# Order of the block products at the quad border, and chunks of two and four FF pairs in the down projection

## Chip, cores, metric

One core of one Trainium2 chip. The metric is device time in microseconds (us) of one execution of the whole program, the median of several runs.

## The reference

One layer of a hybrid decoder on 512 prompt positions and 64 sample positions (8 sequences of 8), 576 columns in all, D_MODEL 2048, D_FF 5632, everything in float32:

```
h = rmsnorm(x); p = h @ w_in                      # 2048 x 5120
y_a = u * (tril(W_s) @ v + b_s); y_b = B * causal_dwconv3(C * x_B)
x = x + concat(group_rmsnorm(y_a), group_rmsnorm(y_b)) @ w_out
h = rmsnorm(x)
gate = causal_dwconv3(h @ w_gate)                 # 2048 x 5632
x = x + (silu(gate) * (h @ w_up)) @ w_down        # 5632 x 2048
y = rmsnorm(x)
```

Besides y the last two rows of each convolution's input and the normalised v of the samples are outputs. The change lies in the last two matrix products, the ConvFFN.

## The kernel before

**Split products.** TensorE multiplies in a rounded 32-bit format, so every float32 operand is split: hi is a rounded copy (ScalarE), lo the rest (VectorE), and each product is three matmuls, hi*hi, hi*lo, lo*hi, always 128x128 weights against 288 columns (HALF of the 576). The weights live in rings of four pieces (`w_hi`, `w_lo`; in the down projection `dw_hi`, `dw_lo`).

**Quads.** The first 4 of the 44 FF tiles are multiplied plainly (`std_quad`). The other 40 go through `quad(i, u)`: one tile of gate and up together by a block scheme with 7 products in place of 8. The 2x2 blocks of weights are a = gate rows of even k (`raw[:, 0]`), b = gate rows of odd k (`raw[:, 1]`), c and d = the same for up (`raw_c`, `raw_d`). VectorE makes the sums: `sum1` = c + d into `raw_e`, `sum2` = raw_e - a, `sum3` = a - c (in place of a), `sum4` = b - raw_e (in place of b). Product t uses `quad_form(t)` against `b_form(t)` and goes to one of four PSUM banks (b, b+1, b+2, b+3); banks of two quads alternate. ScalarE copies bank b after the first product that stands alone in it (`snap`, semaphore s1_done) and bank b+1 (into `up_sum`, s5_done) before later products add to them. `form_hi` (L1030) and `form_lo` (L1555) are the splits. Each is issued in a hand-written order on its engine:

- ScalarE `quad` (L1096): hi of forms 3 to 6 between silu, copies and the hi of the activations (`act_hi`), then hi of the next quad's forms 0, 1, 2.
- VectorE `quad` (L1660): `up2`, `c21`, lo 3, `sum3`, `times_gate`, act sums, lo 4, act_lo, lo 5, zpad, lo 6, act_lo, zpad, `sum1` of the next quad, `gate_conv`, lo 0, lo 1, `sum2`, lo 2, `sum4`.
- SyncE `quad_loads` (L446): raw_c when all four sums of the quad before are done, raw[:, 1] after its split 4, raw_d after split 5, raw[:, 0] after split 6. The very first quad loads raw[:, 0] early and, once std_quad 3 is half done, raw_c, raw_d, raw[:, 1].
- GpSimd (L618 to L674): the split activations of an FF pair (two tiles) are stored to DRAM (`act_scratch`) in four rounds per pair, in the seven forms that the down projection needs.

**Down projection.** It is the same 7-product scheme with the FF pairs as inner dimension. `CHUNKS` lists (first pair, number of pairs) of six chunks; each chunk has 8 visits, one for each two output tiles. Visit v makes 7 products of n pairs (n x 3 matmuls each), so 63 matmuls with three pairs and 84 with four. Each chunk needs seven activation forms, loaded from DRAM by GpSimd into 12 slots (`load_form`, L676, n x 288 KB each), and each visit a weight block loaded by SyncE (L475, n x 256 KB) into one of two buffers (`down_buf`; visit 0 has its own, `down_v0`, in the place of raw_e and after it). GpSimd makes the first and third weight sum (`sums13`, L690), VectorE the second and fourth (`down_s2`, `down_s4`) and seven splits `down_lo` (L1712); five VectorE instructions read the banks out (L1741 to L1770). From chunk 1 on GpSimd also adds copied banks to X (`snap_add`).

At the border between the last quad and visit 0 GpSimd issues the seven loads of forms as their slots come free:

```
for k, n in ((0, 1), (1, 1), (4, 2), (6, 2), (2, 3), (3, 3), (5, 4)):
    load_form(k, piece_done, N_LAST + n)
store_act(PAIRS - 1, 0)
sums13(0)
```

and SyncE the weights of visit 0 after split 4 of the last quad (`lo_ready >= N_LAST + 5`), those of visit 1 after split 6. In visit 0 TensorE also transposes the state rows (`states_t`, L2144), ScalarE copies them (`rows_stage`, L1148), and GpSimd writes them out ahead of its sums of visit 2 (L719). Forms 7 and 8 of the next chunk are loaded at visit 1, forms 9, 10, 11 at visit 2, 12 and 13 at visit 7, and the last pair's activations are stored at visits 2, 4, 6.

Of the kernel before, what the change touches and what calls it, by code (L numbers as in the profile page):

```python
# [22 lines left out]
F32R = mybir.dt.float32r  # L23
ALU = mybir.AluOpType
# [6 lines left out]
def build_layer(nc, x_prompt, x_sample, state_conv_mix, state_conv_ffn, norm_mix_g, w_in, sgu_norm_g,  # L31
# [21 lines left out]
    CHUNKS = ((0, 3), (3, 3), (6, 4), (10, 4), (14, 4), (18, 4))  # L53
# [16 lines left out]
    with ctx:  # L70
# [104 lines left out]
        slots = [sb(f"form{n}", [P, JM, 2, HALF], F32R, at=h_at + n * SLOT) for n in (0, 1, 2, 3, 9, 10, 8, 7, 6, 4, 5, 11)]  # L175
# [190 lines left out]
        def quad_form(t):  # L366

            return (raw[:, 0], raw_e[:, :, :], raw[:, 1], raw_e[:, :, :], raw[:, 1], raw_d[:, :, :], raw[:, 0])[t]
# [26 lines left out]
        def _(sp):  # L395
# [79 lines left out]
            for v in range(VISITS * len(CHUNKS)):  # L475
                f0, n, g = visit(v)
                if v == 0:
                    sp.wait_ge(stage_b_out, 16 * (PAIRS - 2))
                    sp.wait_ge(lo_ready, N_LAST + 5)
                else:  # L480
                    sp.wait_ge(lo_ready, D0 + NQ * (v - 1))
# [15 lines left out]
        def _(pool):  # L497
# [192 lines left out]
            def sums13(v):  # L690

                pool.wait_ge(down_landed[v % 2], 16 * (v // 2 + 1))
                if v == 1:
                    pool.wait_ge(piece_done, D0)
                g.tensor_tensor(down_sum(v), down_form(v, 6), down_form(v, 5), ALU.add).then_inc(s13_ready, 1)
# [16 lines left out]
            for k, n in ((0, 1), (1, 1), (4, 2), (6, 2), (2, 3), (3, 3), (5, 4)):  # L712
                load_form(k, piece_done, N_LAST + n)
            store_act(PAIRS - 1, 0)
            sums13(0)
            rows_ffn(FT - 1)
            for v in range(VISITS * len(CHUNKS)):
                ch, gv = v // VISITS, v % VISITS
                if v == 1:  # L719
                    pool.wait_ge(rows_staged, 1)  # L720
                    g.dma_start(new_ffn_prompt[0, 0].rearrange("r (t c) -> (r t) c", c=P), ffn_stage[0:2 * FT, 0, :]).then_inc(rows_out, 16)
                    rows = new_ffn_sample[0].rearrange("b k (t c) -> (b k t) c", c=P)
                    g.dma_start(rows[0:5 * P, :].rearrange("(n p) c -> p n c", p=P), ffn_stage[:, 1:6, :]).then_inc(rows_out, 16)
                    g.dma_start(rows[5 * P:2 * NB * FT, :], ffn_stage[0:2 * NB * FT - 5 * P, 6, :]).then_inc(rows_out, 16)
                    g.dma_start(new_mix_prompt[0, 0].rearrange("r (t c) -> (r t) c", c=P), mix_stage[0:16, 0, :]).then_inc(rows_out, 16)
                    g.dma_start(new_mix_sample[0].rearrange("b k (t c) -> (b k t) c", c=P), mix_stage[:, 1, :]).then_inc(rows_out, 16)
                if v == 2:
                    pool.wait_ge(rows_out, 5 * 16)
# [1518 lines left out]
```

## Time and profile before

| | |
|---|---|
| time, median of 3 runs | 2348.78 us (2340.26 to 2353.99) |
| the profiled execution | 2352.12 us |
| its span, first to last instruction | 2350.4 us, TensorE clock 0.99 granted |
| busy: TensorE, weight loads | 97%, 96% |
| busy: VectorE, ScalarE, GpSimd | 72%, 41%, 24% |
| quads | 888.9 to 1795.2 us |
| chunks 0, 1 of the down projection | 1803.4 to 1887.7, to 1955.5 us |
| DMA, mean | 136 GB/s |

Times are from the start of the span. Matmuls overlap in the profile: each is shown with some 0.29 us, while the next starts 0.13 us later, so a stretch is read by its length and the number of matmuls in it, not by busy time. PE is TensorE, DVE VectorE, ACT ScalarE, POOL GpSimd, SPq SyncE's queue of DMA issues. An engine's idle time is given before the instruction that it ended with, and what released it.

### The profile page before, as it was taken

To read this page: it belongs to the slowest core of one execution; us is meant where nothing else is said; L and a number is where in the kernel's file an instruction comes from. 1 tells how busy PE (TensorE), PEld (TensorE's weight loads), DVE (VectorE), ACT (ScalarE), POOL (GpSimd) and SP (SyncE) were. 2 spreads that over 40 slices of the span, in tenths; PEclk is the share of its full clock that TensorE was granted. 3 is DMA by queue.
4 is the path that set the end of the run, shared out by engine and by line. 5 is a ranking of instruction groups with operands and counts; after the bars stand their busy time and mean duration, and the time that the engine had idled before them with its cause. 6 is when DMAs were issued, how large, how long until landed. Compare 5 with 4: busy or idle time off the path is not lost. (4 is left out here: it accounts for less than half of the span.)

```text
span 2350.4 us, 43938 instructions
## 1 busy us (share of the span) xinstructions
PE 2276.6 (97%) x16978; PEld 2259.5 (96%) x16978; DVE 1688.3 (72%) x2281; ACT 971.4 (41%) x1469; POOL 555.5 (24%) x641
## 2 busy tenths in 40 slices
PE   7999999999999899999999999999998899999995
PEld 7999999999999899999999999999997899999995
DVE  6357744446322768787888888888886799888896
ACT  6224321223111444454444444444443454444454
POOL 2310000000222001111011111111113267656685
PEclk9999999999999999999999999999999999999998
DMA  7322233223433243534444344443435566765522
GB/s 245 98 81 60 73 86 90 75 86 112 155 105 101 73 137 115 163 116 149 129 140 155 113 158 129 135 147 127 152 123 210 175 218 223 235 204 191 175 86 99
DMA packets 368936, 320.09 MB, mean 136 GB/s; under 512 B 8648, under 2 KB 348739, under 8 KB 363072
## 3 DMA queue, kind: packets, MB, share of 16 engines
q1 hardware_dynamic: 346320, 203.98, 29.6%
q0 software_dynamic: 22512, 114.69, 13.0%
q8 instruction: 69, 1.13, 0.2%
q14 instruction: 35, 0.29, 0.0%
HBM read 258.32 MB, written 60.31 MB: 136 GB/s over the span
## 5 line engine op out<-in xcount | busy, mean ns | idle before, releaser
L1827 PE MATMUL ps<-h_hi,w_hi 128*128 128x288 f32 x1792 | 532.7, 297 | 2.2 <-issue 2.0
L1829 PE MATMUL ps<-h_hi,w_lo 128*128 128x288 f32 x1792 | 529.1, 295 | 0.0
L1828 PE MATMUL ps<-h_lo,w_hi 128*128 128x288 f32 x1792 | 528.9, 295 | 0.0
L2167 PE MATMUL ps<-form,dw_hi 128*128 128x288 f32 x1232 | 369.6, 300 | 23.6 <-DVE dw_lo L1715 21.0
L2168 PE MATMUL ps<-form,dw_hi 128*128 128x288 f32 x1232 | 365.0, 296 | 0.0
L2169 PE MATMUL ps<-form,dw_lo 128*128 128x288 f32 x1232 | 364.3, 296 | 0.0
L1827 PEld LDWEIGHTS ps<-h_hi,w_hi 128*128 128x128 f32 x1792 | 337.3, 188 | 3.5 <-issue 2.7
L1828 PEld LDWEIGHTS ps<-h_lo,w_hi 128*128 128x128 f32 x1792 | 337.2, 188 | 0.0
L1829 PEld LDWEIGHTS ps<-h_hi,w_lo 128*128 128x128 f32 x1792 | 337.1, 188 | 0.0
L1223 DVE TENSOR_TENSOR w_lo<-raw,w_hi 128x1024 fp32r<-128x1024 f32 x128 | 162.8, 1301 | 205.9 <-ACT w_hi L785 205.8
L1715 DVE TENSOR_TENSOR dw_lo<-down,dw_hi 128x512 fp32r<-128x512 f32 (+1 forms) x282 | 258.3, 928 | 51.9 <-ACT dw_hi L799 48.0
L2108 PE MATMUL ps<-hq,w_hi 128*128 128x288 f32 x960 | 286.0, 298 | 7.9 <-DVE w_lo L1560 7.8
L2109 PE MATMUL ps<-hq,w_hi 128*128 128x288 f32 x960 | 283.8, 296 | 0.0
L2110 PE MATMUL ps<-hq,w_lo 128*128 128x288 f32 x960 | 282.8, 295 | 0.0
L2167 PEld LDWEIGHTS ps<-form,dw_hi 128*128 128x128 f32 x1232 | 233.0, 189 | 27.6 <-issue 16.5
L2168 PEld LDWEIGHTS ps<-form,dw_hi 128*128 128x128 f32 x1232 | 234.9, 191 | 0.0
L2169 PEld LDWEIGHTS ps<-form,dw_lo 128*128 128x128 f32 x1232 | 234.6, 190 | 0.0
L785 ACT ACTIVATE w_hi<-raw 128x1024 fp32r<-128x1024 f32 x128 | 132.0, 1055 | 246.1 <-PE ps L1829 227.8
L1560 DVE TENSOR_TENSOR w_lo<-raw,w_hi 128x1024 fp32r<-128x1024 f32 x160 | 195.0, 1219 | 23.2 <-ACT w_hi L1043 23.2
L799 ACT ACTIVATE dw_hi<-down 128x512 fp32r<-128x512 f32 (+1 forms) x282 | 165.6, 593 | 110.2 <-PE ps L2169 88.2
L1043 ACT ACTIVATE w_hi<-raw 128x1024 fp32r<-128x1024 f32 x160 | 168.9, 1055 | 98.7 <-DMA raw<-in_w_gate_dram 70.7
L623 POOL DMA_DIRECT2D act_scratch<-stage x68 | 45.6, 670 | 642.5 <-DVE stage L1528 633.2
(289 smaller groups left out, 5195.3 us busy)
## 6 DMA issues: line engine op xcount, KB each, us to landing
raw<-in_w_gate_dram SPq DMA_DIRECT2D x88, 512.0 KB, 4.5
raw<-in_w_in_dram SPq DMA_DIRECT2D x80, 512.0 KB, 4.1
down<-in_w_down_dram SPq DMA_DIRECT2D x32, 1024.0 KB, 5.5
form<-act_scratch POOLq DMA_DIRECT2D x28, 1152.0 KB, 7.2
act_scratch<-stage POOLq DMA_DIRECT2D x46, 576.0 KB, 4.6
raw_c<-in_w_up_dram SPq DMA_DIRECT2D x40, 512.0 KB, 3.8
raw_d<-in_w_up_dram SPq DMA_DIRECT2D x40, 512.0 KB, 5.3
raw<-in_w_out_dram SPq DMA_DIRECT2D x32, 512.0 KB, 4.0
```

The lines of the kernel that those rows point to most:

```text
L1043: a.activation(w_hi[:, c], quad_form(t), ACT.Copy).then_inc(hi_ready, 1)
L1560: v.tensor_tensor(w_lo[:, c], quad_form(t), w_hi[:, c].bitcast(F32), ALU.subtract).then_inc(lo_ready, 1)
L1715: v.tensor_tensor(dw_lo[:, m % 4, 0:n], down_form(m // NQ, m % NQ), dw_hi[:, m % 4, 0:n].bitcast(F32), ALU.subtract).then_inc(lo_ready, 1)
L1827: te.matmul(out, whi, xhi, start=start, stop=False)
L1828: te.matmul(out, whi, xlo, start=False, stop=False)
L1829: return te.matmul(out, wlo, xhi, start=False, stop=stop)
L2108: te.matmul(out, w_hi[:, c, j, :], b_form(t, 0, j), start=start and j == 0, stop=False, skip_group_check=True)
L2109: te.matmul(out, w_hi[:, c, j, :], b_form(t, 1, j), start=False, stop=False, skip_group_check=True)
L2110: last = te.matmul(out, w_lo[:, c, j, :], b_form(t, 0, j), start=False, stop=stop and j == PJ - 1, skip_group_check=True)
L2167: te.matmul(out, dw_hi[:, m % 4, j, :], act_f[:, j, 0, :], start=start and j == 0, stop=False, skip_group_check=True)
L2168: te.matmul(out, dw_hi[:, m % 4, j, :], act_f[:, j, 1, :], start=False, stop=False, skip_group_check=True)
L2169: last = te.matmul(out, dw_lo[:, m % 4, j, :], act_f[:, j, 0, :], start=False, stop=stop and j == n - 1, skip_group_check=True)
```

## The change

Five things. (1) In a quad the first product is b's (`raw[:, 1]`, bank b+2), then a's and (c+d)'s; `sum1`, `sum2`, `sum4` follow in VectorE's order, `sum3` moves from behind split 3 to behind split 4 and, in even quads, act_lo and act_t4. SyncE's code of the quads is the same. (2) At the border SyncE asks for visit 0's weights after split 3 and `sum4`; GpSimd loads forms 0 and 1 and holds the other five until those weights have landed; the two sums of visit 0 are made by VectorE in the last quad, and `down_lo(3)` comes ahead of the last gate products. The first four slots are numbered so that forms 0 and 1 lie where b's product has read. (3) Chunks 0 and 1 have 2 and 4 pairs instead of 3 and 3: a visit has 42 and 84 matmuls, forms are 576 and 1152 KB, weights 512 and 1024 KB. (4) The state rows are transposed in visit 2 and written out in visit 4. (5) Forms 9, 10, 11 are loaded at visits 3, 4, 5, one each, and the last activations stored at visits 1, 3, 5.

```diff
@@ -50,7 +50,7 @@
     VISITS = KT // 2
-    CHUNKS = ((0, 3), (3, 3), (6, 4), (10, 4), (14, 4), (18, 4))
+    CHUNKS = ((0, 2), (2, 4), (6, 4), (10, 4), (14, 4), (18, 4))
@@ -172,7 +172,7 @@
         SLOT = JM * 2 * HALF * 4
-        slots = [sb(f"form{n}", [P, JM, 2, HALF], F32R, at=h_at + n * SLOT) for n in (0, 1, 2, 3, 9, 10, 8, 7, 6, 4, 5, 11)]
+        slots = [sb(f"form{n}", [P, JM, 2, HALF], F32R, at=h_at + n * SLOT) for n in (2, 3, 0, 1, 9, 10, 8, 7, 6, 4, 5, 11)]
@@ -365,7 +365,7 @@
-            return (raw[:, 0], raw_e[:, :, :], raw[:, 1], raw_e[:, :, :], raw[:, 1], raw_d[:, :, :], raw[:, 0])[t]
+            return (raw[:, 1], raw[:, 0], raw_e[:, :, :], raw_e[:, :, :], raw[:, 1], raw_d[:, :, :], raw[:, 0])[t]
@@ -476,9 +476,8 @@
                     sp.wait_ge(stage_b_out, 16 * (PAIRS - 2))
-                    sp.wait_ge(lo_ready, N_LAST + 5)
-                else:
-                    sp.wait_ge(lo_ready, D0 + NQ * (v - 1))
+                    sp.wait_ge(sum_done, 4 * (FT - STD) - 1)
+                sp.wait_ge(lo_ready, N_LAST + 4 if v == 0 else D0 if v == 1 else D0 + NQ * (v - 1))
@@ -692,6 +691,7 @@
                     pool.wait_ge(piece_done, D0)
+                    pool.wait_ge(s13_ready, 2)
@@ -709,24 +709,14 @@
             pool.wait_ge(stage_b_out, 16 * 2)
-            for k, n in ((0, 1), (1, 1), (4, 2), (6, 2), (2, 3), (3, 3), (5, 4)):
+            for k, n in ((0, 1), (1, 1), (2, 2), (3, 2), (4, 3), (5, 4), (6, 3)):
+                if k == 2:
+                    pool.wait_ge(down_landed[0], 16)
...
-            sums13(0)
...
-                if v == 1:
-                    pool.wait_ge(rows_staged, 1)
-                    g.dma_start(new_ffn_prompt[0, 0].rearrange("r (t c) -> (r t) c", c=P), ffn_stage[0:2 * FT, 0, :]).then_inc(rows_out, 16)
...
-                    g.dma_start(new_mix_sample[0].rearrange("b k (t c) -> (b k t) c", c=P), mix_stage[:, 1, :]).then_inc(rows_out, 16)
-                if v == 2:
-                    pool.wait_ge(rows_out, 5 * 16)
-                    g.memset(facc[:, :], 0.0).then_inc(facc_done, 1)
@@ -738,6 +728,17 @@
                     sums13(v + 1)
+                if v == 4:
+                    pool.wait_ge(rows_staged, 1)
+                    g.dma_start(new_ffn_prompt[0, 0].rearrange("r (t c) -> (r t) c", c=P), ffn_stage[0:2 * FT, 0, :]).then_inc(rows_out, 16)
...
+                    g.dma_start(new_mix_sample[0].rearrange("b k (t c) -> (b k t) c", c=P), mix_stage[:, 1, :]).then_inc(rows_out, 16)
+                if v == 5:
+                    pool.wait_ge(rows_out, 5 * 16)
+                    g.memset(facc[:, :], 0.0).then_inc(facc_done, 1)
@@ -747,12 +748,10 @@
                         load_form(k, piece_done, N_LAST + 5)
-                if v == 2:
-                    for k in (9, 10):
-                        load_form(k, lo_ready, D0 + 2 * NQ)
-                    load_form(11, piece_done, N_LAST + 4)
-                if v in (2, 4, 6):
-                    store_act(PAIRS - 1, v // 2)
+                elif 3 <= v <= 5:
+                    load_form(v + 6, lo_ready, D0 + 2 * NQ)
+                if v in (1, 3, 5):
+                    store_act(PAIRS - 1, (v + 1) // 2)
@@ -1032,14 +1031,12 @@
                 act.wait_ge(piece_done, n - 3)
-                if t == 0:
-                    act.wait_ge(raw_landed[0], a_landed(i, u))
-                elif t == 2:
-                    act.wait_ge(raw_landed[1], a_landed(i, u))
+                if t < 2:
+                    act.wait_ge(raw_landed[1 - t], a_landed(i, u))
...
-                    act.wait_ge(sum_done, sums(i, u, {1: 1, 3: 2, 4: 3, 6: 4}[t]))
+                    act.wait_ge(sum_done, sums(i, u, {2: 1, 3: 2, 4: 3, 6: 4}[t]))
@@ -1102,13 +1099,13 @@
                     silu(q - 1)
-                act.wait_ge(piece_done, n + 1)
+                act.wait_ge(piece_done, n + 2)
...
-                act.wait_ge(piece_done, n + 2)
+                act.wait_ge(piece_done, n + 3)
@@ -1186,10 +1183,10 @@
                 bank_snap(v, 2, 3, bank_a, u2_snap)
-                if v == 0:
+                if v == 2:
...
-                elif v in (2, 4, 6):
-                    act_hi(PAIRS - 1, v // 2)
+                if v in (1, 3, 5):
+                    act_hi(PAIRS - 1, (v + 1) // 2)
@@ -1574,15 +1571,15 @@
-                dve.wait_ge(lo_ready, first_piece(i, u) + 2)
+                dve.wait_ge(lo_ready, first_piece(i, u) + 3)
...
+                dve.wait_ge(sum_done, sums(i, u, 3))
+                v.tensor_tensor(raw[:, 0], raw[:, 0], raw_c[:, :, :], ALU.subtract).then_inc(sum_done, 1)
+
+            def sum4(i, u):
...
-                v.tensor_tensor(raw[:, 0], raw[:, 0], raw_c[:, :, :], ALU.subtract).then_inc(sum_done, 1)
-
-            def sum4(i, u):
-                dve.wait_ge(lo_ready, first_piece(i, u) + 3)
@@ -1596,7 +1593,6 @@
                     form_lo(1, 0, 1)
-                    sum2(1, 0)
@@ -1619,6 +1615,7 @@
                     form_lo(1, 0, 2)
+                    sum2(1, 0)
@@ -1667,7 +1664,6 @@
                 form_lo(i, u, 3)
-                sum3(i, u)
@@ -1678,8 +1674,9 @@
                     act_t4(j)
+                sum3(i, u)
...
-                dve.wait_ge(piece_done, n + 3)
+                dve.wait_ge(piece_done, n + 2)
@@ -1691,8 +1688,10 @@
                                 ALU.add).then_inc(z_ready, 1)
-                if not last:
-                    sum1(*nxt)
+                if last:
+                    dve.wait_ge(down_landed[0], 16)
+                    v.tensor_tensor(down_sum(0), down_form(0, 6), down_form(0, 5), ALU.add).then_inc(s13_ready, 1)
+                    v.tensor_tensor(down_form(0, 6), down_form(0, 0), down_form(0, 6), ALU.subtract).then_inc(s13_ready, 1)
@@ -1702,9 +1701,10 @@
                     form_lo(*nxt, 0)
+                    sum1(*nxt)
...
+                    form_lo(*nxt, 2)
...
-                    form_lo(*nxt, 2)
@@ -1734,9 +1734,9 @@
             c21(FT - 1, 4)
+            down_lo(3)
...
-            down_lo(3)
@@ -1800,9 +1800,9 @@
                     down_s4(vi + 1)
-                if vi in (2, 4, 6):
-                    act_lo(PAIRS - 1, vi // 2)
-                    if vi == 2:
+                if vi in (1, 3, 5):
+                    act_lo(PAIRS - 1, (vi + 1) // 2)
+                    if vi == 1:
@@ -2090,10 +2090,10 @@
-                if t in (0, 2, 4):
-                    return hq[:, (0, 1, 3)[t // 2], part, j, :]
-                if t in (1, 3):
-                    return tq[:, t // 2, part, j, :]
+                if t in (0, 1, 4):
+                    return hq[:, {0: 1, 1: 0, 4: 3}[t], part, j, :]
+                if t in (2, 3):
+                    return tq[:, t - 2, part, j, :]
@@ -2118,11 +2118,11 @@
                     pe.wait_ge(quad_read, q - (STD + 1))
-                product(i, u, 0, b, True, False)
+                product(i, u, 0, b + 2, True, True)
+                product(i, u, 1, b, True, False)
...
-                product(i, u, 1, b + 1, True, False)
-                product(i, u, 2, b + 2, True, True)
+                product(i, u, 2, b + 1, True, False)
@@ -2184,9 +2184,9 @@
                 j = 2 * (vi % VISITS)
-                if vi == 1:
+                if vi == 3:
...
-                elif vi > LAST_V:
+                if vi > LAST_V:
@@ -2200,7 +2200,8 @@
                 down_product(vi, 3, ba, False, False)
-                if vi == 0:
+                if vi == 2:
+                    pe.wait_ge(bank_read, 8)
```

## Rows read from the trace of the kernel before

**Rows 1.** The page, part 1: busy us, share of the span, instructions.
```profile
PE 2276.6 (97%) x16978; PEld 2259.5 (96%) x16978; DVE 1688.3 (72%) x2281; ACT 971.4 (41%) x1469; POOL 555.5 (24%) x641
```

**Rows 2.** Windows: stretch, us, busy us (x) of PE, PEld, DVE, ACT, POOL; PEclk, DMA share, GB/s.
```profile
888.87:1795.18 906.31, 898.40 (x6722) 895.11 (x6720) 751.50 (x994) 435.10 (x595) 113.68 (x204) 1.00 0.45 142
1772.83:1795.18 22.35, 22.35 (x170) 22.29 (x168) 15.66 (x22) 8.09 (x12) 6.01 (x10) 1.00 0.68 270
1795.18:1803.38 8.20, 0.18 (x2) 0.00 (x0) 0.84 (x1) 0.90 (x2) 1.46 (x2) 0.78 0.93 319
1803.38:1887.65 84.27, 73.32 (x513) 71.72 (x514) 66.31 (x124) 40.15 (x91) 28.55 (x35) 0.94 0.46 160
1826.73:1835.06 8.33, 8.33 (x66) 8.33 (x64) 6.39 (x14) 5.03 (x11) 3.86 (x5) 1.00 0.45 148
1887.65:1955.48 67.83, 67.83 (x506) 67.27 (x505) 66.94 (x109) 36.97 (x80) 46.41 (x45) 1.00 0.55 190
1967.63:2212.34 244.71, 244.58 (x1850) 244.37 (x1849) 218.00 (x311) 117.23 (x220) 156.28 (x136) 1.00 0.64 210
```

**Rows 3.** Waits of PE from 888 to 1795: us in total, times, longest us.
```profile
PE ps L2108 <- DVE w_lo L1560: 7.8, 12, 1.9
```

**Rows 4.** Timeline of SyncE: issues in one quad and for the first quad.
```profile
877.35 1.18 SPq L450 DMA_DIRECT2D raw<-in_w_gate_dram  x1
...
1667.06 0.37 SPq L450 DMA_DIRECT2D raw_c<-in_w_up_dram  x1
1669.84 0.37 SPq L450 DMA_DIRECT2D raw<-in_w_gate_dram  x1
...
1674.61 0.37 SPq L450 DMA_DIRECT2D raw<-in_w_gate_dram  x1
```

**Rows 5.** Timelines of DVE, ACT and PE: the same quad's end, the next's beginning.
```profile
1673.36 1.22 DVE L1560 TENSOR_TENSOR w_lo<-raw,w_hi 128x1024 fp32r<-128x1024 f32 x1
...
1680.09 1.06 ACT L1043 ACTIVATE w_hi<-raw 128x1024 fp32r<-128x1024 f32 x1 [2.61 <-DMA raw<-in_w_gate_dram]
...
1681.34 1.22 DVE L1560 TENSOR_TENSOR w_lo<-raw,w_hi 128x1024 fp32r<-128x1024 f32 x1
...
1682.61 0.40 PE L2108 MATMUL ps<-hq,w_hi 128*128 128x288 f32 x1 [0.38 <-DVE w_lo L1560]
```

**Rows 6.** Chain that ended last, 1800 to 1850: start us, us, what.
```profile
1783.18 18.66 DMA down_v<-in_w_down_dram
...
1803.99 0.24 PE ps L2168
...
1808.67 2.30 issue
...
1817.75 2.81 DVE down L1726
...
1832.24 13.01 DMA down<-in_w_down_dram
```

**Rows 7.** DMA: packets of 1779.5 to 1802.1 and 1671.0 to 1681.6; one load alone.
```profile
DMA packets 2502, 8.22 MB, mean 364 GB/s; under 512 B 160, under 2 KB 1455, under 8 KB 2502
...
DMA packets 3383, 2.74 MB, mean 258 GB/s; under 512 B 80, under 2 KB 3127, under 8 KB 3383
...
down<-in_w_down_dram SPq DMA_DIRECT2D x1, 768.0 KB, 4.7
```

**Rows 8.** Timelines of POOL and DVE at the border and beside each other.
```profile
1779.52 2.12 POOL L680 DMA_DIRECT2D form<-act_scratch  x4
...
1802.48 0.84 DVE L1715 TENSOR_TENSOR dw_lo<-down_v,dw_hi 128x384 fp32r<-128x384 f32 x1 [10.28 <-ACT dw_hi L799]
...
1810.32 1.49 DVE L1715 TENSOR_TENSOR dw_lo<-down_v,dw_hi 128x384 fp32r<-128x384 f32 x3
...
1818.14 1.02 POOL L695 TENSOR_TENSOR down_s<-down 128x384 f32<-128x384 f32 x1
...
1932.83 2.91 DVE L1715 TENSOR_TENSOR dw_lo<-down,dw_hi 128x384 fp32r<-128x384 f32 x3
```

More of the change, by code:

```diff
@@ L718, in _ @@
                 ch, gv = v // VISITS, v % VISITS
-                if v == 1:
-                    pool.wait_ge(rows_staged, 1)
-                    g.dma_start(new_ffn_prompt[0, 0].rearrange("r (t c) -> (r t) c", c=P), ffn_stage[0:2 * FT, 0, :]).then_inc(rows_out, 16)
[L722 to L725, printed above, removed]
-                    g.dma_start(new_mix_sample[0].rearrange("b k (t c) -> (b k t) c", c=P), mix_stage[:, 1, :]).then_inc(rows_out, 16)
-                if v == 2:
-                    pool.wait_ge(rows_out, 5 * 16)
-                    g.memset(facc[:, :], 0.0).then_inc(facc_done, 1)
                 if ch == X2_CHUNK + 1:
@@ L740, in _ @@
                     sums13(v + 1)
+                if v == 4:
+                    pool.wait_ge(rows_staged, 1)
+                    g.dma_start(new_ffn_prompt[0, 0].rearrange("r (t c) -> (r t) c", c=P), ffn_stage[0:2 * FT, 0, :]).then_inc(rows_out, 16)
+                    rows = new_ffn_sample[0].rearrange("b k (t c) -> (b k t) c", c=P)
+                    g.dma_start(rows[0:5 * P, :].rearrange("(n p) c -> p n c", p=P), ffn_stage[:, 1:6, :]).then_inc(rows_out, 16)
+                    g.dma_start(rows[5 * P:2 * NB * FT, :], ffn_stage[0:2 * NB * FT - 5 * P, 6, :]).then_inc(rows_out, 16)
+                    g.dma_start(new_mix_prompt[0, 0].rearrange("r (t c) -> (r t) c", c=P), mix_stage[0:16, 0, :]).then_inc(rows_out, 16)
+                    g.dma_start(new_mix_sample[0].rearrange("b k (t c) -> (b k t) c", c=P), mix_stage[:, 1, :]).then_inc(rows_out, 16)
+                if v == 5:
+                    pool.wait_ge(rows_out, 5 * 16)
+                    g.memset(facc[:, :], 0.0).then_inc(facc_done, 1)
                 if v >= VISITS:
@@ L1575, in sum2 @@
             def sum2(i, u):
-                dve.wait_ge(lo_ready, first_piece(i, u) + 2)
+                dve.wait_ge(lo_ready, first_piece(i, u) + 3)
                 v.tensor_tensor(raw_e[:, :, :], raw_e[:, :, :], raw[:, 0], ALU.subtract).then_inc(sum_done, 1)
             def sum3(i, u):
-                dve.wait_ge(sum_done, sums(i, u, 2))
+                dve.wait_ge(sum_done, sums(i, u, 3))
                 v.tensor_tensor(raw[:, 0], raw[:, 0], raw_c[:, :, :], ALU.subtract).then_inc(sum_done, 1)
             def sum4(i, u):
-                dve.wait_ge(lo_ready, first_piece(i, u) + 3)
+                dve.wait_ge(sum_done, sums(i, u, 2))
                 v.tensor_tensor(raw[:, 1], raw[:, 1], raw_e[:, :, :], ALU.subtract).then_inc(sum_done, 1)
```

## The prediction, made before the changed kernel ran

> **What bounds the kernel now.** The page first: TensorE is busy 97% of 2350.4 us, so a change counts only where TensorE stands still [rows 1]. Then the busy time by stretch [rows 2], read through the count of matmuls. A gate/up quad (one tile of both products, 7 block products of 24 matmuls) lasts 22.35 us when nothing waits; a visit of the down projection with three FF pairs (63 matmuls) 8.33 us, which is 0.132 us a matmul; with four pairs 244.71 / 22 = 11.1 us. Against these the stretches show what is lost:
> - 40 quads, 906.31 us, less 40 x 22.35 = 894.0: **12.3 us**.
> - the border, last quad to first visit: **8.2 us**.
> - chunk 0 (visits 0 to 7), 84.27 us, less 8 x 8.33 and about 1.2 us for the nine state transposes: **16.4 us**.
> - chunk 1, 67.83 less 66.6: **1.2 us**, and some 1.0 at the first visit of chunk 2.
> Together 39 us. Chunks 2 to 4 lose nothing and the last one is not touched.
>
> Who is late there. In the quads TensorE waits for VectorE's weight split, twelve times, 7.8 us as idle time [rows 3]. One case in order of time [rows 4, 5]: the last split of the quad ends at 1674.58, only then SyncE asks for raw[:,0] (1674.61); ScalarE could start on it at 1680.09, VectorE's split starts at 1681.34, and the matmuls due at 1682.04 start at 1682.61. At the border the chain shows one transfer, down_v, 18.66 us from issue to use [rows 6]. The queues say why: 8.22 MB pass in 22.6 us at 364 GB/s, seven form loads of 864 KB ahead of the weights [rows 7]. In visit 4 it is the same picture, 13.01 us for a weight load with three form loads beside it [rows 6]; alone such a load takes 4.7 us [rows 7].
>
> **Quads.** The new order is raw[:,1], raw[:,0], c+d. raw[:,1] is free after the fifth split (1669.84), almost 5 us before raw[:,0] [rows 4], and raw[:,0], requested last as before, is now due one product (3.2 us) later. The 0.6 us typical lateness is thus covered. What is given up: sum3 moves from behind the fourth split to behind the fifth (and in even quads behind act_lo and act_t4). SyncE's raw_c load waits for it and the three others queue behind that. In the quad of rows 4 and 5 sum3 is what releases raw_c at 1667.06; now it ends about 5 us later, at 1672.0, so four loads of 512 KB and an activation store run together from 1672. Rows 7 show 2.74 MB moved in 10.6 us at 258 GB/s with two such loads and two stores; four loads (2.1 MB) and 1.2 MB of stores at 300 to 400 GB/s need 8 to 11 us, so raw[:,0] lands at 1681 to 1683 in place of 1680.06. With 1.05 + 1.22 us for the two splits it is ready by 1683.3 to 1685.3, and it is due at 1685.2. Covered, with 0 to 2 us to spare: not every stall goes. Bounds: all 12.3 us gained, or none. I take 8, since the usual case is covered and the worse ones (longest 1.9 us) are those of slow transfers. The snapshots of banks b and b+1 now have one product between them and the product that adds to the bank, 3.2 us against 0.4 us of copying: nothing. In even quads the second waits for act_lo at T+11 with T+12.8 its limit: still nothing.
>
> In the first quad raw[:,1] is requested third, at 877.35 [rows 4], and now wanted first. The third in a bunch lands some 6 us later (883.9; raw[:,0] of rows 4 and 5 took 5.4); with two splits it is ready at 886.2, due at 888.87. ScalarE's copies of the last standard gate tile are queued behind it and come some 2 us later than now, and VectorE's convolution, gate products and third and fourth splits after them; by the same durations the fourth split ends at 897.6, due at 888.87 + 9.6 = 898.5. Bounds 0 and 2 us lost; I take 0.
>
> **Border.** Forms 0 and 1 (two pairs, 576 KB) start as before at 1779.5 [rows 8]. The weights are released by the fourth split and sum4, about 1780.4, not 1783.2, and have 1.2 MB beside them instead of 6: at 364 GB/s (1.7 MB) they land at 1786. GpSimd holds forms 2 to 6 until then. These (2.95 MB), weights 1 (0.52) and a store (0.59) are 4.1 MB, 10 to 11 us: all there by 1797 to 1798, form 2 by 1790. Splits 0 to 2 can be done before the quad ends at 1795.18, the two sums have moved to VectorE, which stands idle for 10.28 us here [rows 8]; behind its new wait for the weights stand the convolution and the splits of visit 0, which need until 1793.5 at most. So the 8.2 us become about 0.5. TensorE then also keeps its full clock: after the idle time the first matmuls came 0.24 us apart, not 0.13 [rows 6], which cost 1.5 us of chunk 0's 16.4. Down_lo(3) ahead of the gate products takes away the 2.30 us before product 3 [rows 6].
>
> **Chunk 0 with two pairs.** TensorE: 8 x 42 x 0.132 = 44.4 us, 1.2 for the transposes (moved to visit 2). But VectorE does not shrink as fast. Its ops per visit: seven splits and two subtractions of 128x256, five PSUM reads of 128x288. Three in a row of 128x384 take 1.49 us with the last one's 0.55, so starts lie 0.47 us apart [rows 8]; by size 0.37 at 288 and about 0.34 at 256: 9 x 0.34 + 5 x 0.37 = **4.9 us** (the same count gives 6.1 for three pairs; the row has 6.39 busy). GpSimd's two sums delay it: beside them three splits took 2.91 us, free of them 1.49 [rows 8]. With 0.7 to 0.9 us each, VectorE needs 4.9 to 6.7 us against TensorE's 5.55. I take 6.2 a visit, between: +5.2 us over eight.
> Transfers: the forms of chunk 1 are now 1152 KB (1.18 MB). Forms 7 and 8 are issued after the sums of visit 2, about 1805.9, with a store behind: 2.95 MB beside the weights of visit 3, requested at the same time. 3.5 MB at 364 to 400 GB/s land by 1815, the visit would start at 1813.8 and needs them 1.5 us earlier: about 3 us lost. Forms 9, 10, 11 now come one a visit, so what visit 4 lost (13.01 instead of 4.7 us for the load) is spread; I put 2 us for them, for the stores (one a visit in 1, 3, 5) and for the five output DMAs ahead of GpSimd's sums of visit 6. Chunk 0: 44.4 + 1.2 + 5.2 + 3 + 2 = **55.8**, bounds 48 (VectorE never late, weights in time) and 71.
>
> **Chunk 1 with four pairs.** 8 x 11.1 = 88.8 (the row with the same visits: VectorE 218.0 of 244.7, no wait), 1.5 for the start: 90.3.
>
> **Sum.** Before, from the end of the quads to the second visit of chunk 2 less its own 11.1: 8.2 + 84.3 + 67.8 + 1.0 = 161.3. After: 0.5 + 55.8 + 90.3 = 146.6, a gain of 14.7; with 8 from the quads 22.7. The profiled execution took 2352.12 us (span 2350.4), so 2329.4; the median of the runs shown is 3.3 lower, which gives **2326**.
>
> A rule against the change: the Trainium skill (SBUF — State Buffer, Who interferes with whom) says of VectorE and GpSimd that one with two SBUF inputs blocks the other entirely for the whole instruction. The one subtraction that took 2.81 us while GpSimd's two sums ran from 1818.14 to 1820.13 agrees [rows 6, 8]. By that rule every visit pays for both sums in full, which is the third rival below.
>
> **Rivals.**
> 1. The quads gain nothing: raw[:,0] comes as late for product 1 as it did for product 0, since sum3 holds the queue back. For it: the loads are bunched. Against: DMA share 0.45 there. 2334. Chance 0.13.
> 2. A two-pair visit runs no faster than a three-pair one (weights or VectorE late each time, 8.4 us): chunk 0 is 8 x 8.4 + 1.2 + 2 = 70.4, the down part gains nothing: 2340. For it: weights took 13 us beside forms. Against: visits 2 and 6 of now have no wait. Chance 0.12.
> 3. VectorE stands still for both sums in each two-pair visit, 4.9 + 2 x 0.9 = 6.7 us: 4 us more: 2330. For it: the 2.81 us. Against: in visit 2 as it is VectorE was busy only 0.3 us over its count [rows 2]. Chance 0.14.
> 4. Slower: the bunched loads make product 1 wait in every quad. Place: raw[:,0] landing more than 1 us after the next quad has begun. To be slower than now in sum the quads must lose over 12.3 + 14.7 = 27 us, 0.7 us a quad; at 1 us each (40 us, 27.7 more than now) it is 2348.8 + 27.7 - 14.7 = 2362. Against: 0 to 2 us of cover by the rows. For it: sum3 comes 5 us later in every quad. Chance 0.05.
> 5. The weights still land behind forms 0 and 1 and the last stores of the quads, and 5 us of the gap stay: 2331. For it: they came last of all before. Against: less than a third of the bytes. Chance 0.06.
> The forecast as it stands, 0.50.
>
> **Numbers.** A measurement of this kernel tells about 0.5% (11.7 us) from no change. Faster by more, below 2337: the forecast, 3, 5, most of 1 = 0.78. Within: 2 and the rest of 1 = 0.16. Slower: 0.06. The range goes from 2314 (all quad stalls gone, chunk 0 in 51) to 2341 (rival 2).
>
> **What would show it.** Right: idle time of L2108 for w_lo near 0 to 4 us; no idle time over 1 us at the border and the matmuls there 0.13 us apart; down_v landed 9 us or more before its first use; two-pair visits 5.6 to 6.7 us with one wait of about 3 us in front of visit 3; four-pair visits 11.1 from the second on. Wrong: idle time in front of each quad's second product; weight loads over 10 us in chunk 0; VectorE with no idle time in chunk 0 and visits over 7 us.

## The result, and the profile after

The changed kernel takes 2374.11 us (median of 4 runs, 2367.53 to 2380.52) against 2350.85 of the kernel before (4 runs): ratio 1.0107, 95% interval 1.0063 to 1.0151. It is slower by about 1%, where the prediction had 2326 us. The profiled execution took 2376.21 us, its span is 2374.5.

The page's part 1 and its row for the quads' matmuls, and the row of part 6 for the gate loads; below it the same row before the change:

```profile
PE 2283.6 (96%) x16978; PEld 2261.5 (95%) x16978; DVE 1687.8 (71%) x2283; ACT 971.9 (41%) x1469; POOL 550.2 (23%) x639
...
L2108 PE MATMUL ps<-hq,w_hi 128*128 128x288 f32 x960 | 288.9, 301 | 34.2 <-DVE w_lo L1557 34.0
...
raw<-in_w_gate_dram SPq DMA_DIRECT2D x88, 512.0 KB, 6.5
```

```profile
raw<-in_w_gate_dram SPq DMA_DIRECT2D x88, 512.0 KB, 4.5
```

The instructions are the same but for two weight sums, which moved from GpSimd to VectorE [rows 1]; what grew is idle time in the quads. A gate load now takes 6.5 us (median) from issue to landing, where it took 4.5. The windows of the same stretches as in [rows 2] (all quads, one quad, chunk 0, chunk 1, 22 visits of chunks 2 to 4), with the same columns:

```profile
889.87:1831.01 941.14, 906.92 (x6723) 898.64 (x6722) 762.16 (x1004) 438.06 (x601) 106.92 (x207) 1.00 0.45 135
...
1618.08:1642.20 24.12, 22.73 (x169) 22.49 (x169) 19.63 (x25) 10.96 (x16) 4.04 (x6) 1.00 0.48 142
...
1831.01:1888.12 57.11, 48.98 (x347) 46.01 (x346) 46.75 (x115) 33.51 (x88) 22.07 (x30) 1.00 0.74 254
1888.12:1978.94 90.82, 90.58 (x673) 90.23 (x674) 82.72 (x117) 43.45 (x82) 57.80 (x50) 0.98 0.53 186
1990.04:2234.70 244.66, 243.34 (x1841) 243.13 (x1840) 215.15 (x307) 116.67 (x220) 155.80 (x136) 1.00 0.62 204
```

| us | before | after | difference | predicted |
|---|---|---|---|---|
| start of the first quad | 888.9 | 889.9 | +1.0 | 0 |
| 40 quads | 906.3 | 941.1 | **+34.8** | -8 |
| border, last quad to visit 0 | 8.2 | 0.0 | -8.2 | -7.7 |
| chunks 0 and 1 | 152.1 | 147.9 | -4.2 | -6.0 |
| first visit of chunk 2 | 12.1 | 11.1 | -1.0 | -1.0 |
| the rest | 382.8 | 384.5 | +1.7 | 0 |

So the border and the down projection gave 13.4 us, close to the 14.7 predicted, and the quads took back two and a half times that.

**Where the quads lose.** The waits of TensorE between 889 and 1832 us (before, 7.8 us in 12 waits [rows 3]):

```profile
PE ps L2108 <- DVE w_lo L1557: 34.0, 32, 2.3
```

By the matmuls' starts, 31 us stand in front of the second product (`raw[:, 0]`) in 22 quads and 8 in front of the first (`raw[:, 1]`) in 11 quads. 29 of these 33 waits are in odd quads, each of which follows an even one, where VectorE puts act_lo and act_t4 ahead of sum3. One of them in order of time: the quad that ends at 1618.08, and the next. SyncE:

```profile
1608.76 0.37 SPq L450 DMA_DIRECT2D raw_c<-in_w_up_dram  x1
1609.38 0.82 SPq L450 DMA_DIRECT2D raw<-in_w_gate_dram  x1
1610.39 1.33 SPq L450 DMA_DIRECT2D raw_d<-in_w_up_dram  x1
1611.90 1.49 SPq L450 DMA_DIRECT2D raw<-in_w_gate_dram  x1
```

VectorE, then ScalarE, in the same stretch (start, length, instruction, and in brackets the idle time before it):

```profile
1607.36 1.22 DVE L1579 TENSOR_TENSOR raw<-raw,raw_c 128x1024 f32<-128x1024 f32 x1
...
1610.00 1.22 DVE L1557 TENSOR_TENSOR w_lo<-raw,w_hi 128x1024 fp32r<-128x1024 f32 x1
...
1621.66 1.23 DVE L1557 TENSOR_TENSOR w_lo<-raw,w_hi 128x1024 fp32r<-128x1024 f32 x1 [2.50 <-ACT w_hi L1040]
```

```profile
1615.71 1.06 ACT L1040 ACTIVATE w_hi<-raw 128x1024 fp32r<-128x1024 f32 x1 [2.33 <-DMA raw<-in_w_gate_dram]
1620.56 1.06 ACT L1040 ACTIVATE w_hi<-raw 128x1024 fp32r<-128x1024 f32 x1 [3.80 <-DMA raw<-in_w_gate_dram]
```

TensorE, the first matmul of the second product:

```profile
1622.94 0.40 PE L2108 MATMUL ps<-hq,w_hi 128*128 128x288 f32 x1 [1.39 <-DVE w_lo L1557]
```

sum3 ends at 1608.6 and releases raw_c; by then the splits that release the other three are done or nearly so, and all four loads, 2 MB, go out within 4.6 us. `raw[:, 0]` lands at 1620.5, 2.4 us after the next quad has begun (1618.08), and the matmuls due at 1621.3 start at 1622.9. Before, the same four requests lay 7.6 us apart (1667.06 to 1674.61 [rows 4]) and the last one landed 5.4 us after its issue began [rows 5]; here it takes 8.6 us, of which the issue itself is 1.5. SyncE's own waits between 900 and 1790 us say it for all quads, after and then before:

```profile
SPq L450 <- DVE raw L1579: 728.6, 38, 21.8
SPq L450 <- DVE w_lo L1557: 25.2, 36, 1.5
```

```profile
SPq L450 <- DVE raw L1582: 600.9, 38, 16.8
SPq L450 <- DVE w_lo L1560: 176.7, 115, 3.0
```

The queue waits 3.4 us more per quad for sum3 ((728.6 - 600.9) / 38), and then hardly at all for the splits that had spaced the loads.

### The profile page after: what moved, and what is told of

The parts are those of the page before. It is cut to its first block and busy times, and to the rows that moved or that the text cites. A ratio compares the mean times of both kernels' runs of the same rounds, so it can differ in the third digit from the quotient of the medians.

```text
span 2374.5 us, 43970 instructions
## 1 busy us (share of the span) xinstructions
PE 2283.6 (96%) x16978; PEld 2261.5 (95%) x16978; DVE 1687.8 (71%) x2283; ACT 971.9 (41%) x1469; POOL 550.2 (23%) x639
## 5 line engine op out<-in xcount | busy, mean ns | idle before, releaser
L2167 PE MATMUL ps<-form,dw_hi 128*128 128x288 f32 x1232 | 367.6, 298 | 13.8 <-DVE dw_lo L1715 10.4
L1715 DVE TENSOR_TENSOR dw_lo<-down,dw_hi 128x512 fp32r<-128x512 f32 (+1 forms) x282 | 252.7, 904 | 54.8 <-ACT dw_hi L798 49.7
L2108 PEld LDWEIGHTS ps<-hq,w_hi 128*128 128x128 f32 x960 | 181.3, 189 | 42.5 <-DVE w_lo L1557 40.9
```

Of the source, the lines that this page charges most:

```text
L1715: v.tensor_tensor(dw_lo[:, m % 4, 0:n], down_form(m // NQ, m % NQ), dw_hi[:, m % 4, 0:n].bitcast(F32), ALU.subtract).then_inc(lo_ready, 1)
L2108: te.matmul(out, w_hi[:, c, j, :], b_form(t, 0, j), start=start and j == 0, stop=False, skip_group_check=True)
L2167: te.matmul(out, dw_hi[:, m % 4, j, :], act_f[:, j, 0, :], start=start and j == 0, stop=False, skip_group_check=True)
```

## The experiments

**1. sum3 back in its old place, all else as changed.** This parts the place of sum3 from the new order of products.

```diff
@@ after, VectorE's quad
                 form_lo(i, u, 3)
+                sum3(i, u)
...
-                sum3(i, u)
                 form_lo(i, u, 5)
```

> The changed kernel with sum3 (a - c) back behind the fourth split, everything else as changed. Theory A (the late sum3 holds back raw_c's load, and SyncE's three other loads of the quad queue behind it, so raw[:,0] lands 2 us after the next quad has begun): raw_c is requested about 4 us earlier, raw[:,0] lands before the quad's beginning, the 40 quads shrink from 941.1 to 895 to 900 us, the whole to 2328 to 2334. Theory B (b's product first, with sum1 behind the first split, is itself what is late): the quads stay over 925 us, the whole over 2358.

Measured: 2328.14 us (4 runs), ratio to before 0.9905 (0.9886 to 0.9924). Windows (quads, chunk 0, chunk 1), and SyncE in one quad:

```profile
888.91:1783.67 894.76, 894.76 (x6723) 894.68 (x6722) 761.53 (x1004) 439.98 (x601) 107.80 (x207) 1.00 0.45 142
1783.67:1840.25 56.58, 48.27 (x348) 45.91 (x346) 47.70 (x115) 33.22 (x88) 21.57 (x30) 1.00 0.68 235
1840.25:1930.77 90.52, 89.49 (x674) 89.05 (x673) 82.71 (x116) 43.30 (x82) 57.63 (x50) 1.00 0.55 194
```

```profile
1612.44 0.37 SPq L450 DMA_DIRECT2D raw_c<-in_w_up_dram  x1
1615.23 0.37 SPq L450 DMA_DIRECT2D raw<-in_w_gate_dram  x1
1618.41 0.37 SPq L450 DMA_DIRECT2D raw_d<-in_w_up_dram  x1
1619.91 0.37 SPq L450 DMA_DIRECT2D raw<-in_w_gate_dram  x1
```

All 46 us are gone: no wait in any quad, 22.37 us each. The place of sum3 is the whole loss, and with it in its old place the change makes the kernel 1% faster. The requests again lie up to 3.2 us apart and each issue takes 0.37 us.

**2. The quads of before with the new down projection.**

```diff
@@ before: quads unchanged; border, visits and chunks of after
-    CHUNKS = ((0, 3), (3, 3), ...
+    CHUNKS = ((0, 2), (2, 4), ...
...
```

> The quads of the kernel before with the changed border and down projection (weights ahead of forms, chunks of 2 and 4 pairs; forms 0 and 1 in the old slots). Both theories: quads 906 us as before, the down part 13 us shorter, the whole 2336 to 2339. If the down part's gain needs the new quads (slots, sum order at the border), a gap of several us stays at the border and the whole is over 2343.

Measured: 2335.69 us, ratio 0.9936 (0.9918 to 0.9953). Quads 901.0, no gap at the border, chunks 0 and 1 together 150.8. The down part alone is worth 10.5 us in this profile (161.3 - 150.8); the same quads lost 12.3 us in the profile of before and 7.0 here, so this loss varies from one execution to another. Against experiment 1, on the same chip, the new order of products is worth 6.2 us of quads (901.0 - 894.8).

**3. sum3 late in the kernel before, and nothing else.**

```diff
@@ before, VectorE's quad
                 form_lo(i, u, 3)
-                sum3(i, u)
...
+                sum3(i, u)
                 form_lo(i, u, 5)
```

> The kernel before with one line moved: sum3 behind the fifth split, as in the change. Theory A: raw[:,0] is late as in the changed kernel but is the first form here, with 3.2 us less cover, so the quads lose over 2 us each: 970 to 1020 us, the whole 2410 to 2465. Theory B: the quads stay within 5 us of 906, the whole 2345 to 2356.

Measured: 2412.6 us, ratio 1.0268 (1.0250 to 1.0286); quads 971.5. TensorE's waits in the quads:

```profile
PE ps L2108 <- DVE w_lo L1560: 51.7, 26, 3.9
```

The same move costs 65 us with the old order of products and 46 with the new one, so late sum3 costs with either order. Not all of it is waiting. Behind 12 of the waits here the granted clock fell and 12 to 15 matmuls lay 0.24 us apart, some 1.6 us each time and 19 us in all; in the changed kernel this happened twice (3.2 us). One such stretch:

```profile
1057.00:1060.00 3.00, 3.00 (x15) 3.00 (x14) 2.93 (x4) 1.83 (x4) 0.00 (x0) 0.51 0.00 0
```

By the matmuls' starts TensorE waits 56.2 us with sum3 late in the old order (10.0 before) and 39.7 in the new one (none in experiment 1). So the product's time (3.2 us) that the new order leaves for `raw[:, 0]` does save waiting, as the prediction said, and the late sum3 eats more than that.

**4. The change, with an eighth of the raw_c load.** Same waits and same four requests at the same places; only 448 KB are missing from the bunch. This kernel leaves out seven eighths of raw_c's weights in all quads but the first, so part of the up product is computed from old data.

```diff
@@ after, SyncE's quad_loads
-                    part(w_up, 0, raw_c[:, :, :], c_landed)
+                    sp.dma_start(raw_c[:, 0:1, :], wpart(w_up, f, 0)[:, 0:1, :]).then_inc(c_landed, 16)
```

> The changed kernel with raw_c's load cut to an eighth (64 of 512 KB, one of eight k rows) in all quads but the first; the rest of raw_c keeps old data, so that part of up is not computed. The time of its request, behind the late sum3, is the same. If raw[:,0] is late because four full loads follow each other in a bunch, it lands about 2 us earlier and the quads fall from 941 to 900 to 912 us, the whole to 2333 to 2346. If the late request itself is what costs (SyncE's place, not the bytes behind it), the quads stay over 930.

Measured: 2325.08 us (2 runs), ratio 0.9925 (0.9900 to 0.9951); quads 894.7, as without any wait. SyncE in one quad:

```profile
1615.04 0.34 SPq L462 DMA_DIRECT2D raw_c<-in_w_up_dram  x1
1615.63 0.42 SPq L450 DMA_DIRECT2D raw<-in_w_gate_dram  x1
1616.22 0.64 SPq L450 DMA_DIRECT2D raw_d<-in_w_up_dram  x1
1617.51 0.37 SPq L450 DMA_DIRECT2D raw<-in_w_gate_dram  x1
```

More came back than was expected. sum3 stands in the same late place and no matmul waits, so its place costs only through the bunch of four full loads behind it. With seven eighths of one load gone, the issues take 0.34 to 0.64 us and not up to 1.49, and the last load lands at 1623.8, 1.9 us before the next quad begins. VectorE's row of sum3 in this quad helps to see why all came back:

```profile
1613.63 1.22 DVE L1579 TENSOR_TENSOR raw<-raw,raw_c 128x1024 f32<-128x1024 f32 x1
```

This quad began at 1603.3: sum3 starts 10.4 us into it, and so in nearly every even quad (about 9.2 in odd ones), while in the changed kernel the means are 12.2 and 12.8. VectorE works in order, so a late `raw[:, 0]` puts off splits 1 and 2 and the sums behind them, and with these sum3 of the same quad, which releases the loads of the next: the lateness is handed on. In the changed kernel the quad from 1595.07 to 1618.08 shows it. TensorE doesn't wait in it, but its `raw[:, 0]` landed 0.3 us after its beginning, and its sum3 starts 12.3 us into it. Whether the bytes or SyncE's issuing is the dearer part of a bunch this run doesn't tell.

**5. sum3 right behind split 4.** Between the two places: as in the change for odd quads, one activation split and one copy earlier for even ones.

```diff
@@ after, VectorE's quad
                 form_lo(i, u, 4)
+                sum3(i, u)
                 if prev and u % 2 == 0:
                     act_lo(j, 1)
                     act_t4(j)
-                sum3(i, u)
```

> The kernel after, with sum3 right behind split 4 of the quad, ahead of act_lo and act_t4 in even quads; half way between the place of the kernel before (behind split 3) and that of the change. In odd quads this is the place of the change, in even quads about 1.5 us earlier. Theory (the quads' loss is the lateness of raw[:,0] behind the loads that sum3 releases): stalls sit in front of the second product of odd quads, which follow even ones; these get most of their time back, so the quads take 897 to 915 us against 941.1 of the change and 894.8 with the early sum3, the whole 2330 to 2348. Rival (any place behind split 4 bunches the four loads alike, and the order of the products is what costs): quads over 925, the whole over 2355.

Measured: 2344.35 us (10 runs), ratio 1.0016 (1.0000 to 1.0032); quads 910.1. TensorE's waits in the quads:

```profile
PE ps L2108 <- ACT up_sum L1112: 5.7, 8, 1.2
PE ps L2108 <- DVE w_lo L1557: 4.4, 6, 1.0
```

sum3 now starts 10.7 us into even quads and 11.2 into odd ones (means), not 12.2 and 12.8. These 1.5 us take away seven eighths of the waits for splits, so the loss is a matter of 1 to 3 us against a due time. A second kind of wait appears, on ScalarE's copy of bank b+1 in even quads: act_lo now stands behind sum3, ScalarE waits for it (`act_ready`) ahead of that copy, and the fifth product waits for the copy. That was not expected; in the changed kernel this wait is there once, with 0.1 us. So both places behind split 4 have a price.

**6. Three and three pairs in place of two and four,** with sum3 early and the new border.

```diff
@@ experiment 1
-    CHUNKS = ((0, 2), (2, 4), (6, 4), (10, 4), (14, 4), (18, 4))
+    CHUNKS = ((0, 3), (3, 3), (6, 4), (10, 4), (14, 4), (18, 4))
```

> As the kernel with sum3 early, but chunks 0 and 1 with three pairs each: of the down part only the weights ahead of forms, the spread loads and the moved rows remain. If the two-pair chunk was needed (its smaller burst at the border), the weights of visit 1 and the last forms come late and chunks 0 and 1 take 150 us or more in place of 147.1: the whole over 2331. If weights ahead of forms alone did it and two pairs only make VectorE the bound (about 11 us over TensorE's 45.6 in chunk 0), chunks 0 and 1 take 139 to 144 us: the whole 2320 to 2325.

Measured: 2321.67 us, ratio 0.9916 (0.9890 to 0.9942). Chunks 0 and 1:

```profile
1782.42:1855.11 72.69, 69.92 (x516) 68.96 (x515) 60.37 (x120) 39.50 (x88) 27.79 (x32) 0.98 0.65 229
1855.11:1923.00 67.89, 67.89 (x507) 67.19 (x506) 67.16 (x109) 36.97 (x80) 46.13 (x45) 1.00 0.56 194
```

```profile
PE ps L2167 <- DMA form<-act_scratch: 2.7, 3, 1.9
```

The two chunks take 140.6 us against 147.1 in experiment 1, and the next visit 12.0 against 11.1: the two and four pairs of the change are 5.6 us dearer than three and three. The ratios of the two overlap (they ran on different chips), so this rests on the stretches alone. What is left of the border's cost stands in visit 0, which takes 13.1 us and not 8.33: 2.7 us of idle time for forms, while the DMA engines are full (408, 306 and 354 GB/s in the three stretches of 3 us from 1783), and behind it matmuls 0.24 us apart at a lower granted clock (0.89 in the third of these stretches).

**7. No hold.** GpSimd requests forms 2 to 6 without waiting for the weights of visit 0.

```diff
@@ experiment 1, GpSimd at the border
-                if k == 2:
-                    pool.wait_ge(down_landed[0], 16)
```

> As the kernel with sum3 early (chunks of 2 and 4), but GpSimd doesn't hold forms 2 to 6 until the weights have landed. 5.8 MB then go as one bunch, 14 to 15 us at 400 GB/s, and the weights of visit 0 land near its end, about when the quads end. If the hold is what removed the 8.2 us: a gap of 4 us or more at the border, the whole 2332 or more. If the smaller forms did most of it: a gap of 0 to 2 us, the whole 2327 to 2331.

Measured: 2329.49 us, ratio 0.9941 (0.9923 to 0.9960); no gap either, chunk 0 57.8, chunk 1 92.4 (56.6 and 90.5 in experiment 1). The weights land 5.4 us after their request though nothing is held: the request goes out 0.1 us after that of form 0, and before the change it came behind five of the seven forms. So the hold isn't what closes the border's gap, and it is worth 3 us at most. What is left is the earlier request and the smaller forms; the earlier request with three-pair forms and no hold was not run. Experiment 6 has no gap with three-pair forms, but it holds them.

**8. The weight sums of visits 1 to 7 on VectorE** in place of GpSimd.

```diff
@@ experiment 1, VectorE, between down_lo(m + 6) and down_lo(m + 7) of visits 0 to 6; w = vi + 1
+    dve.wait_ge(down_landed[w % 2], 16 * (w // 2 + 1))
+    v.tensor_tensor(down_sum(w), down_form(w, 6), down_form(w, 5), ALU.add).then_inc(s13_ready, 1)
+    v.tensor_tensor(down_form(w, 6), down_form(w, 0), down_form(w, 6), ALU.subtract).then_inc(s13_ready, 1)
```

> As the kernel with sum3 early, but the two weight sums of visits 1 to 7 are made by VectorE (0.34 us each by the spacing at 128x256) and not by GpSimd, which keeps its waits. If VectorE's standing still beside GpSimd's sums is what makes product 3 of visits 2, 4 and 6 wait (2.2, 1.5 and 2.4 us), these go and chunk 0 falls from 56.6 to 50 to 53 us: the whole 2321 to 2326. If the transfers bound chunk 0, it stays over 55: the whole 2326 to 2331.

Measured: 2324.03 us, ratio 0.9925 (0.9904 to 0.9946). Chunk 0, and VectorE's splits in it, first of this run and then of the changed kernel:

```profile
1782.32:1834.49 52.17, 47.80 (x347) 45.83 (x346) 47.18 (x129) 33.36 (x88) 10.28 (x16) 1.00 0.73 258
...
L1719 DVE TENSOR_TENSOR dw_lo<-down,dw_hi 128x256 fp32r<-128x256 f32 (+1 forms) x43 | 18.3, 438 | 4.5 <-ACT dw_hi L802 4.5
```

```profile
L1715 DVE TENSOR_TENSOR dw_lo<-down,dw_hi 128x256 fp32r<-128x256 f32 (+1 forms) x43 | 22.0, 530 | 8.7 <-ACT dw_hi L798 8.5
```

VectorE does 14 instructions more (x129 against x115) and is busy for 47.2 us against 47.7 in experiment 1; chunk 0 is 4.4 us shorter. So the two sums of a visit cost VectorE about as much time when GpSimd makes them as when it makes them itself. The Trainium skill (SBUF — State Buffer, Who interferes with whom) says that a VectorE instruction with two SBUF inputs contends with a GpSimd instruction that reads SBUF, and that the one of the two which holds the shared ports blocks the other fully; the split's mean of 530 ns beside GpSimd's sums against 438 without them agrees.

The expectation was right in its number and only in part in its reason. The waits of the fourth products did not go: by the matmuls' starts they are 1.7, 1.1 and 0.6 us in visits 2, 4 and 6, where experiment 1 has 2.2, 1.5 and 2.4. Of the 4.4 us, 2.2 are waits in front of the first two products of visit 6, which experiment 1 has and this run hasn't. How much comes from VectorE's standing still and how much from GpSimd's own order of work, this run doesn't part.

**9. Experiments 6 and 8 together,** to see whether they add up.

```diff
@@ experiment 8
-    CHUNKS = ((0, 2), (2, 4), (6, 4), (10, 4), (14, 4), (18, 4))
+    CHUNKS = ((0, 3), (3, 3), (6, 4), (10, 4), (14, 4), (18, 4))
```

> The two versions that gained most put together: sum3 early again, weights ahead of forms at the border, chunks 0 and 1 of three pairs each, and the two weight sums of visits 1 to 7 on VectorE. Theory (with three pairs VectorE needs 6.1 + 0.9 = 7.0 us a visit against TensorE's 8.33, so it has room; what is left in chunk 0 of the three-pair version, 72.7 us against 67.8, is mostly visit 0, whose products 4 to 6 wait for splits beside GpSimd's sums of visit 1): chunk 0 takes 69 to 71 us, quads 894.7, the whole 2316 to 2321. Rival (visit 0's waits come from transfers, or VectorE itself becomes late): chunk 0 at 72 or more, the whole 2321 or more.

Measured: 2321.27 us (6 runs), ratio 0.9919 (0.9904 to 0.9934); chunk 0 71.4, chunk 1 68.3, the next visit 12.3. They hardly do: chunk 0 gains 1.3 us on experiment 6. The waits are

```profile
PE ps L2176 <- DMA form<-act_scratch: 3.0, 2, 1.9
```

for the last two of the forms that TensorE waits for in experiment 6, at 419, 415 and 276 GB/s in the stretches of 3 us from 1783. With three pairs visits 1 and 3 to 7 take 8.33 us, so VectorE has room and the sums' place hardly matters; what is left beside the transposes is visit 0 (11.8 us), where TensorE waits for forms. That is the rival's cause, at a time between the two expectations. The kernels of experiments 6 and 9 are both faster than the kernel before and the changed one.

## Why the prediction was wrong

**Quads: the step that failed** is the cover for `raw[:, 0]`: "raw[:,0] lands at 1681 to 1683 ... it is ready by 1683.3 to 1685.3, and it is due at 1685.2. Covered, with 0 to 2 us to spare". Set against the quad above, counted from the end of the quad in which the loads are asked for if nothing waits (1682.0 there, 1595.07 + 22.37 = 1617.4 here):
- request of raw_c: predicted 10.0 us ahead, measured 8.7. sum3 starts 12.3 us into the quad. Undisturbed it is 10.4 (experiment 4), earlier than the 11.1 that the prediction's times give; the rest is VectorE's lateness behind a late `raw[:, 0]`.
- raw_c's request to `raw[:, 0]`'s landing: predicted 9 to 11 us (its own working gives 8 to 11), measured 11.7. The rate was lower than the 300 to 400 GB/s taken (3.28 MB in that time are 280), and SyncE's issues of 0.8 to 1.5 us postpone the last request. Rows 4 had one of 1.18 us in the first bunch at 877.35; it was cited for its time and not priced.
- landing to matmul: 2.3 us from its two splits, measured 2.5.

Together the weights are ready 5.5 us after that point (-8.7 + 11.7 + 2.5), where 1.3 to 3.3 were predicted and 3.2 is due. Even undisturbed, with the request 10.7 us ahead, it would be 3.5 by the same figures (an estimate), a little too late, and the lateness that is handed on makes it worse. The step took "0 to 2 us to spare", a difference of two estimates of some 10 us, as cover, and asked neither how wrong it could be nor what a small miss does to the next quad. The term was put at 8 us gained, with no gain as its lower bound, and it was a loss of 34.8.

Also missed: `raw[:, 1]`, now wanted first. The text said it is free "almost 5 us before raw[:,0]", but it cannot be requested before raw_c, which waits for sum3; so its early freedom was no use, and 11 quads wait for it (8 us). Requesting `raw[:, 1]` ahead of raw_c was not tried.

**Rival 4 was the right one,** with its place (landing over 1 us after the next quad began; 2.4 us in the quad shown), its mechanism (experiments 1, 3 and 4) and nearly its size: 1 us a quad was assumed for 2362 us, and (941.1 - 894.7) / 40 = 1.2 us came. It is not every quad that waits for `raw[:, 0]`, though, but 22 of 40, 18 of them odd ones. It had a chance of 0.05. The rows spoke for it more than that: both ends of the estimate lay within 2 us of the due time.

**First quad: right.** Predicted 0; it starts at 889.9, and the other runs with the new order start between 887.5 and 889.8.

**Border: right.** Predicted 0.5, measured 0.0. GpSimd's hold and the weights, in the trace after (SyncE, then GpSimd):

```profile
1817.78 0.38 SPq L481 DMA_DIRECT2D down_v<-in_w_down_dram  x1
```

```profile
1817.69 1.08 POOL L679 DMA_DIRECT2D form<-act_scratch  x2
1823.22 2.61 POOL L679 DMA_DIRECT2D form<-act_scratch  x5 [4.45 <-DMA down_v<-in_w_down_dram]
```

The weights land 5.2 us after their issue, not 18.66 [rows 6], and 8 us ahead of visit 0. Experiment 7 shows that the hold is not needed for this.

**Chunk 0: right in sum (55.8 predicted, 57.1 measured), partly by chance.** For the 5.2 us of VectorE beside GpSimd's sums, experiment 8 gives 4.4 back, not all of it by that cause. The 3 us for the weights of visit 3 were not there: these land 3.5 us after their request. A smaller loss of this kind comes one visit later: the weights of visit 4, with forms 7 and 8 beside them, land 8.3 us after their request, and 1.5 us stand in front of its first two products. Besides, the fourth products of visits 2 and 4 wait 2.2 and 1.5 us for splits. In visit 2, GpSimd and VectorE:

```profile
1846.94 0.73 POOL L695 TENSOR_TENSOR down_s<-down 128x256 f32<-128x256 f32 x1
1847.63 0.96 POOL L696 TENSOR_TENSOR down<-down 128x256 f32<-128x256 f32 x1
```

```profile
1845.16 0.75 DVE L1525 TENSOR_TENSOR stage<-ue,stage 128x576 fp32r<-128x576 f32 x1
1846.01 0.46 DVE L1540 TENSOR_TENSOR ue<-ue 128x288 f32<-128x288 f32 x1
...
1847.11 2.10 DVE L1715 TENSOR_TENSOR dw_lo<-down,dw_hi 128x256 fp32r<-128x256 f32 x3
```

Three splits take 2.10 us here; at 0.42 us each, with starts 0.34 us apart, they would be near 1.1. But 1.7 of the 2.2 us stay when VectorE makes the sums (experiment 8). Just ahead of these splits VectorE makes an activation split and a copy of the last pair (1845.16 and 1846.01, 1.2 us), which the change moved to visits 1, 3 and 5; the waits stand in the visits behind these. The prediction priced nothing for them on VectorE, and no run takes them away. So rival 3's mechanism was part of the forecast's own term, and rival 2 (visits of 8.4 us) fell: they take 5.8 to 8.8, 7.1 in the mean.

**Chunk 1: right.** 90.3 predicted, 90.8 measured, 13.1 us for its first visit and 11.1 for each other. Still, the two chunks of two and four pairs were the dearer choice: with three and three, visits and border together take 5.6 us less (experiment 6).

**The rest:** +1.7 us where 0 was expected, of which 1.3 is one wait for a form at 2079; the other runs have 382.7 to 384.2.

**The sum.** Against the profiled execution the forecast was 2329.4, and 2376.21 came: 46.8 us more, of which 42.8 are the quads (941.1 in place of 898.3), 1.3 the down part (147.9 in place of 146.6), 1.0 the start and 1.7 the rest. Experiment 1 is what the forecast described, the change with quads that nearly never wait: 2328.1 us against 2326.

## What to carry to other kernels

When an instruction that releases a queue is moved back, write down when the last load behind it will land and what it must be in time for, and treat a margin smaller than the error of that estimate as a wait. Loads that several releases kept apart are part of a schedule: once they go out together each is later, the last most of all. And a change of several parts should be timed part by part: here one line that costs 46 us hid 22 to 25 us of gain from the others (22 by the medians on one chip, 2350.28 and 2328.14; 25 by the spans of the two profiles, 2350.4 and 2325.4).

## What the runs showed of the hardware

- SyncE's issue of a 512 KB load took 0.37 us where the requests lay 1.5 us or more apart (the quad of experiment 1), and 0.8, 1.3 and 1.5 us for the second to fourth of a bunch (the quad of the changed kernel). The median over the 80 gate loads of the quads was 0.83 us against 0.37, the longest 3.2 against 0.92. With one of the four cut to 64 KB it was 0.34 to 0.64 in the quad shown.
- The four bunched loads and the stores beside them moved at 280 GB/s with the DMA engines' share at 0.9 and more; at the border, with form loads, stretches of 3 us reached 408 to 419 GB/s (experiments 6 and 9). The Trainium skill (DMA: Bandwidth & Descriptors, Queues, rings and completion order) says each engine takes turns between queues a packet at a time; no run here separates that from the packets' size.
- TensorE's clock: in two quads of the changed kernel, after idle times of 1.9 and 2.3 us, the granted clock was about 0.6 over the next 3 us. After some four matmuls 0.13 us apart (2.4 GHz) came 14 that lay 0.24 us apart (1.2 GHz), which cost 1.6 us each time:

```profile
1151.10:1154.10 3.00, 2.99 (x14) 2.99 (x15) 2.93 (x3) 0.78 (x2) 0.00 (x0) 0.59 0.00 0
1294.27:1297.30 3.03, 3.02 (x15) 3.02 (x16) 2.96 (x3) 0.81 (x2) 0.00 (x0) 0.62 0.00 0
```

After the other 30 waits, of up to 1.6 us, the matmuls lay 0.13 us apart from the second on. The length of the idle time alone doesn't decide: the clock did not fall after 1.9 us in the kernel before (at 1094.61), nor after 2.8 and 3.3 us in experiment 3 (at 1396.77 and 1106.35), where it fell after 12 other waits of 1.8 to 3.9 us.
